# Turning the weights of a step before the product two steps back, in a differential-attention stage

## The chip, the cores and the metric

The kernel runs on one core of a Trainium2 chip. The metric is the device time of one execution in microseconds. The time before is 4780.38 us, the median of three runs (4776.41 to 4782.08).

## The reference, cut to what matters

One layer of a streaming encoder: a combined input projection, a convolution with a state-space scan, differential attention, a mixing projection, a product-key retrieval and a final norm. The change lies in the attention alone, which is this, for 8 heads, 1024 prompt frames and 32 sample frames (these with 512 cached keys and values):

```
def diff_scores_apply(q, k, v, q_pos, k_pos, lam):
    s = jnp.einsum('bqhjd,bkhjd->bhjqk', q, k).astype(jnp.float32) * (A_DK ** -0.5)
    dist = jnp.abs(q_pos[:, None] - k_pos[None, :]).astype(jnp.float32)
    bias = -alibi_slopes()[:, None, None, None] * dist
    mask = (k_pos[None, :] // CHUNK) <= (q_pos[:, None] // CHUNK)
    a = jax.nn.softmax(jnp.where(mask, s + bias, NEG_INF), axis=-1)
    w = a[:, :, 0] - lam * a[:, :, 1]
    return jnp.einsum('bhqk,bkhd->bqhd', w.astype(v.dtype), v)
```

Each head has two score maps (j = 0, 1); their two softmaxes are subtracted to one matrix w of weights, which multiplies the values. All is float32.

## The kernel before, in words

The program is a row of stages, each closed by a barrier of all engines (`Stage.__exit__`): constants, projection and scan, attention (`differential_attention`), then `retrieve_and_finish`. The attention's output rows go to a scratch tensor in memory, and the last stage's first loads are issued behind the barrier.

In the attention stage every engine runs a loop of its own, with four passes of two heads (b = 0, 1). A pass has STEPS = 18 steps m. In a head, steps n = m % 9 from 0 to 7 are the eight tiles of 128 prompt frames, with (n + 1) * 128 keys each, so the tiles grow from 128 to 1024 keys; n = 8 is the sample tile, 32 frames with 544 keys. A step goes through these parts, for which the text below has short names:

- S(m), `scores` on TensorE (L1342; L1348 and L1349 for the sample tile): the two score maps into PSUM. S holds one tile for each map, so the scores of map j wait until VectorE has read map j of the step before (`biased[j]`).
- B(m), `bias_and_max` on VectorE (L1214, L1218): bias, running maximum, copy to SBUF.
- E(m), `exps` on ScalarE (L1260): the two exponentials and their sums.
- W(m), `combine` on VectorE (L1226, L1228, L1233): the weights w. The last instruction (L1233) waits for the product of step m - 2 (`o_done`), because w has two buffers.
- T(m), `weights_turned` on TensorE (L1360): w is transposed in blocks of 128, in groups of up to four blocks; each group has one of two PSUM tiles, `tp`. It waits for W(m) and, before each group, until ScalarE has emptied that `tp` tile.
- C(m), `weights_out` on ScalarE (L1273, L1275): each group is copied from `tp` to `wT` in SBUF. It waits for T(m) and for the product of step m - 1 (`o_done`), because `wT` has two buffers.
- P(m), `product` on TensorE (L1376): wT times the values into `ob`. It waits for C(m).
- O(m), `o_to_rows` on ScalarE (L1295): `ob` to the output rows.

The keys of each head also are transposed, for the output and the cache: `keys_turned` on TensorE, called K here (four groups through the same two `tp` tiles: two of eight prompt blocks in all at L1324, one small at L1326, one of cached keys at L1329), emptied by `keys_out` on ScalarE (L1284, L1286, L1288). K of the first head stands at the start of a pass, K of the second at m = 8, ahead of S(9).

The order of the work on an engine is its program's order. VectorE: for each m, B(m), then W(m - 1). The other two, before the change:

```
TensorE, step m:  [K if m = 8]  S(m+1)  P(m-2)  T(m-1)
ScalarE, step m:  E(m)  [keys_out if m = 8]  O(m-2)  C(m-1)
```

S is called only while m + 1 < 18, so the last three steps of a pass (m = 17, 18, 19) have no scores on TensorE, and in m = 19 only P(17) and O(17) are left.

Of the kernel before, what the change touches and what calls it, by code (L numbers as in the profile page):

```python
# [1065 lines left out]
def differential_attention(nc, io, dr, c, negdist):  # L1066
# [4 lines left out]
    STEPS = 2 * NT  # L1071
# [17 lines left out]
    with Stage(nc, "attn") as s:  # L1089
# [33 lines left out]
        def step_of(i, m, ahead=1):  # L1123

            return i * STEPS + (m + ahead)

        def turn_val(i, j, ahead=1):
            return i * TURNS + (j // 2 + ahead)

        with nc.Block() as block:  # L1130

            @block.gpsimd
            def _(pool):
                pool.iota(iot[:], [[-1, SEQ]], base=SEQ - P, channel_multiplier=1).then_inc(dist_i, 1)
                with pool.Fori(0, H // 2) as i:
                    for b in range(2):

                        pool.wait_ge(head_used[b], i + 1)
                        pool.sem_inc(gate, 1)
                        col = i * (2 * P) + b * P  # L1140
                        pool.dma_start(qT[b][:], dr["chan"][bass.ds(col, P), :]).then_inc(head_in[b], 16)
                        pool.dma_start(kT[b][:], dr["chan"][bass.ds(col + C_K, P), :]).then_inc(head_in[b], 16)
                        cols = bass.ds(col, P)
                        pool.dma_start(vt[b][:, 0:NPT, :], io["v_prompt_out"].rearrange("(t p) c -> p t c", p=P)[:, :, cols]
                                       ).then_inc(head_in[b], 16)
                        pool.dma_start(vt[b][0:DEC, NPT, :], io["v_sample_out"][:, cols]).then_inc(head_in[b], 16)
                        pool.dma_start(kc[b][:], io["cache_k2"].rearrange("(t p) c -> p t c", p=P)[:, :, cols]
                                       ).then_inc(head_in[b], 16)
                        pool.dma_start(vc[b][:], io["cache_v2"].rearrange("(t p) c -> p t c", p=P)[:, :, cols]
                                       ).then_inc(head_in[b], 16)  # L1150
# [95 lines left out]
            @block.scalar  # L1246
            def _(act):
                for b in range(2):
                    act.sem_inc(head_used[b], 1)
                    act.sem_inc(turn_out[b], 1)  # L1250
                act.sem_inc(o_out, 2)
                act.wait_ge(lam_step, 2)
                act.activation(le[:], ld[:], ACT.Exp).then_inc(lam_exp, 1)

                def exps(i, m):
                    p = m % 2
                    r, W = (P, (m % NT + 1) * P) if m % NT < SAMPLE else (DEC, PAST + DEC)
                    act.wait_ge(ntop_done, step_of(i, m))
                    for j in range(2):
                        act.activation(e[j][p][0:r, 0:W], e[j][p][0:r, 0:W], ACT.Exp, bias=ntop[p][0:r, j:j + 1],  # L1260
                                       scale=AK ** -0.5, accum_out=tot[p][0:r, j:j + 1]).then_inc(exp_done[j], 1)

                def weights_out(i, m):
                    r = P if m % NT < SAMPLE else DEC
                    for g, blocks in enumerate(groups(m % NT)):
                        j = turn_of["w", m, g]
                        act.wait_ge(turned[j % 2], turn_val(i, j))

                        act.wait_ge(o_done, step_of(i, m, 2))
                        full = [q for q in blocks if q[1] == P]  # L1270
                        if full:
                            f = len(full)
                            act.activation(wT[j % 2][:, 0:f, 0:r], tp[j % 2][:, 0:f, 0:r], ACT.Copy).then_inc(turn_out[j % 2], 1)  # L1273
                        else:
                            act.activation(wT[j % 2][0:DEC, 0, 0:r], tp[j % 2][0:DEC, 0, 0:r], ACT.Copy).then_inc(turn_out[j % 2], 1)  # L1275

                def keys_out(i, b):

                    act.wait_ge(stored[b], (i + 1) * 64)
                    for g in range(4):  # L1280
                        j = turn_of["k", b, g]
                        act.wait_ge(turned[j % 2], turn_val(i, j))
                        if g < 2:
                            a = act.activation(krow[b][:, 4 * g:4 * g + 4, :], tp[j % 2][:], ACT.Copy)  # L1284
                        elif g == 2:
                            a = act.activation(krow[b][0:DEC, NPT, :], tp[j % 2][0:DEC, 0, :], ACT.Copy)  # L1286
                        else:
                            a = act.activation(kcT[b][:].rearrange("p (t k) -> p t k", k=P), tp[j % 2][:], ACT.Copy)  # L1288
                        a.then_inc(turn_out[j % 2], 1)

                def o_to_rows(i, m):
                    n, b = m % NT, m // NT
                    r = P if n < SAMPLE else DEC
                    act.wait_ge(o_done, step_of(i, m, 3))
                    act.activation(orow[b][0:r, n, :], ob[m % 2][0:r, 0:P], ACT.Copy).then_inc(o_out, 1)  # L1295
                    if n == SAMPLE:
                        act.sem_inc(head_used[b], 1)

                with act.Fori(0, H // 2) as i:
                    keys_out(i, 0)  # L1300
                    for m in range(STEPS + 2):
                        if m < STEPS:
                            exps(i, m)
                        if m == NT - 1:
                            keys_out(i, 1)
                        if m >= 2:
                            o_to_rows(i, m - 2)
                        if 1 <= m <= STEPS:
                            weights_out(i, m - 1)

            @block.tensor
            def _(pe):
# [19 lines left out]
                def scores(i, m):  # L1332
                    b, n = m // NT, m % NT
                    for j in range(2):

                        hold(pe, pe_gate, biased[j], step_of(i, m))
                        half = slice(AK * j, AK * j + AK)
                        if n < SAMPLE:
                            W = (n + 1) * P
                            for k in range(0, W, 512):  # L1340
                                x = min(W, k + 512)
                                mm = pe.matmul(S[j][:, k:x], qT[b][half, n * P:(n + 1) * P], kT[b][half, k:x],  # L1342
                                               start=True, stop=True)
                        else:
                            jj = turn_of["k", b, 3]

                            hold(pe, pe_gate, turn_out[jj % 2], turn_val(i, jj, 2))
                            pe.matmul(S[j][0:DEC, 0:PAST], qT[b][half, SEQ:T], kcT[b][half, :], start=True, stop=True)  # L1348
                            mm = pe.matmul(S[j][0:DEC, PAST:PAST + DEC], qT[b][half, SEQ:T], kT[b][half, SEQ:T],  # L1349
                                           start=True, stop=True)  # L1350
                        mm.then_inc(scored[j], 1)

                def weights_turned(i, m):
                    r = P if m % NT < SAMPLE else DEC
                    pe.wait_ge(w_done, step_of(i, m, 3))
                    for g, blocks in enumerate(groups(m % NT)):
                        j = turn_of["w", m, g]
                        hold(pe, pe_gate, turn_out[j % 2], turn_val(i, j))
                        for k, (blk, size) in enumerate(blocks):
                            t = pe.transpose(tp[j % 2][0:size, k, 0:r], w[m % 2][0:r, blk * P:blk * P + size],  # L1360
                                             c.ident[0:r, 0:r])
                        t.then_inc(turned[j % 2], 1)
# [17 lines left out]
                with pe.Fori(0, H // 2) as i:  # L1380
                    keys_turned(i, 0)
                    scores(i, 0)
                    for m in range(STEPS + 2):
                        if m == NT - 1:
                            keys_turned(i, 1)
                        if m + 1 < STEPS:
                            scores(i, m + 1)
                        if m >= 2:
                            product(i, m - 2)
                        if 1 <= m <= STEPS:  # L1390
                            weights_turned(i, m - 1)


def attend(nc, io, dr, c):
# [1358 lines left out]
```

## Time and profile before

| | |
|---|---|
| median of three runs | 4780.38 us (4776.41 to 4782.08) |
| the profiled execution's own time | 4776.41 us |
| its span in the profile | 4774.6 us |
| mean granted TensorE clock over the span | 0.959 of full speed |
| busy over the span: TensorE, VectorE, ScalarE, GpSimd | 89%, 65%, 21%, 31% |
| attention stage | about 1293 to 1609 us of the span |

How to read it: times inside the span are counted from its start, in microseconds. Busy shares over the whole span are an average over stages with different limits, so the stage of the change is read by itself. A line of the timeline gives the start, the duration and the engine of an instruction, or of a run of equal instructions merged into one (x is how many), and in brackets how long the engine stood idle before it and what ended the wait. A float32 matmul has two records. The ends of matmuls are modelled, so an end can lie a tenth of a microsecond behind the start of the next matmul.

### The profile page before, as it was taken

The numbers are of one execution on the slowest core, as the hardware profiler recorded it, in microseconds if no ns is written. First come the engines' busy times: TensorE is split into PE (matmuls) and PEld (weight loads), VectorE is DVE, ScalarE is ACT, GpSimd is POOL, SyncE is SP. The second block draws the span as 40 slices with busy tenths as digits, with TensorE's granted clock in tenths as the row PEclk, the third lists the DMA queues.
The fourth block names the chain that finished last, engine by engine and source line by source line (L and its number), as shares of the span: only waits on it lengthen the run. The fifth ranks groups of instructions, "written<-read, shape, count | busy, mean of one in ns | idle before, by whom it ended". The sixth has DMA issues, their size and how long they took to land.

```text
span 4774.6 us, 50482 instructions
## 1 busy us (share of the span) xinstructions
PE 4259.6 (89%) x16837; PEld 2648.3 (55%) x16837; DVE 3115.7 (65%) x7131; ACT 996.6 (21%) x2577; POOL 1473.6 (31%) x1391
## 2 busy tenths in 40 slices
PE   7999999999899789988888999878988888888978
PEld 7999777888765675445444555423433433434432
DVE  3444113666377438887788777677777777777784
ACT  2222111234266201111111111111212111212212
POOL 1100001222111003444444344443444444444442
PEclk8999999999899999999999999999999999999999
DMA  2223222344322359999999999999999999999996
GB/s 93 69 88 124 88 90 82 116 132 131 103 82 81 116 188 357 395 413 408 417 406 406 399 419 408 416 420 398 407 409 418 384 404 417 398 412 407 384 414 254
DMA packets 310424, 1379.13 MB, mean 289 GB/s; under 512 B 37856, under 2 KB 112336, under 8 KB 175024
## 3 DMA queue, kind: packets, MB, share of 16 engines
q0 software_dynamic: 167728, 1166.48, 60.5%
q1 hardware_dynamic: 142464, 209.70, 12.7%
q8 instruction: 128, 2.10, 0.2%
q14 instruction: 104, 0.85, 0.0%
HBM read 1295.58 MB, written 80.49 MB: 288 GB/s over the span
## 4 chain that ended last, share of the span: by engine, by line
PE 31%; DMA 20%; DVE 10%; issue 4%; POOL 1%; ACT 0%; SPq 0%; DVEq 0%; ACTq 0%; POOLq 0%
DMA peer_uv<-in_peer_uv_dram,peer_idx 20%; PE peer_acc L2655 18%; PE peer_fo L2596 4%; PE peer_fo L2609 2%; PE peer_fo L2508 2%; DVE peer_uv L1954 2%; PE peer_tb L2461 2%; DVE peer_diag L1984 1%; POOL peer_uv L1821 1%; PE peer_fo L2518 1%; DVE peer_hot L1912 1%; DVE peer_hot L1915 1%; DVE peer_sel L1918 1%; PE peer_sb L2471 0%; DVE peer_pos L1902 0%
## 5 line engine op out<-in xcount | busy, mean ns | idle before, releaser
L2655 PE MATMUL peer_acc<-peer_uv,peer_diag 128*128 128x512 f32 (+1 forms) x4000 | 1932.1, 621 | 300.9 <-DVE peer_diag L1984 294.3
L1821 POOL DMA_INDIRECT peer_uv<-in_peer_uv_dram,peer_idx x1056 | 1224.9, 1160 | 1718.0 <-PE peer_acc L2655 1598.3
L1954 DVE CUSTOM_DVE_ANT_0 peer_uv<-peer_uv,peer_h 128x1024 f32<-128x1024 f32 x1056 | 1290.5, 1222 | 636.8 <-DMA peer_uv<-in_peer_uv_dram,peer_idx 633.4
L2655 PEld LDWEIGHTS peer_acc<-peer_uv,peer_diag 128*128 128x128 f32 (+1 forms) x4000 | 741.5, 194 | 1281.8 <-issue 726.3
L2420 ACT ACTIVATE peer_ge<-peer_pre 128x1 f32<-128x1 f32 x1056 | 212.7, 203 | 2425.1 <-DVE peer_pre L1954 2413.6
L2596 PE MATMUL peer_fo<-peer_space 128*128 128x256 f32 (+2 forms) x1152 | 395.1, 475 | 43.4 <-DVE peer_space L2048 18.3
L99 PE MATMUL proj_bank<-proj_hTh,proj_wplead 128*128 128x352 f32 x1008 | 357.1, 354 | 0.0
L1984 DVE TENSOR_SCALAR peer_diag<-ident,peer_ge,peer_gw 128x128 f32<-128x128 f32 x968 | 332.2, 343 | 10.3 <-ACT peer_ge L2420 8.2
L2596 PEld LDWEIGHTS peer_fo<-peer_space 128*128 128x128 f32 x1152 | 220.7, 196 | 204.9 <-issue 158.2
L100 PE MATMUL proj_bank<-proj_hTr,proj_wplead 128*128 128x352 f32 x1008 | 328.1, 326 | 0.0
L101 PE MATMUL proj_bank<-proj_hTh,proj_wprest 128*128 128x352 f32 x1008 | 328.0, 325 | 0.0
L99 PEld LDWEIGHTS proj_bank<-proj_hTh,proj_wplead 128*128 128x128 f32 x1008 | 192.7, 191 | 23.0 <-issue 22.4
L89 DVE CAST proj_wplead<-proj_wp 128x4096 fp32r<-128x4096 f32 (+1 forms) x14 | 31.0, 2217 | 260.8 <-DMA proj_wp<-in_w_in_dram 126.2
L100 PEld LDWEIGHTS proj_bank<-proj_hTr,proj_wplead 128*128 128x128 f32 x1008 | 192.3, 191 | 15.6 <-issue 15.6
L101 PEld LDWEIGHTS proj_bank<-proj_hTh,proj_wprest 128*128 128x128 f32 x1008 | 192.0, 191 | 0.0
L2609 PEld LDWEIGHTS peer_fo<-peer_space 128*128 128x128 f32 (+1 forms) x1152 | 141.2, 185 | 66.0 <-issue 61.2
L2609 PE MATMUL peer_fo<-peer_space 128*128 128x128 f32 (+1 forms) x1152 | 147.8, 279 | 19.5 <-DVE peer_space L2061 9.9
L2461 PEld LDWEIGHTS peer_tb<-peer_hT,peer_wq 128*128 128x128 f32 x1152 | 146.1, 200 | 32.0 <-issue 29.2
L759 ACT ACTIVATE proj_stg<-proj_bank 128x352 f32<-128x352 f32 (+2 forms) x117 | 57.7, 495 | 486.5 <-PE proj_bank L101 486.5
L2461 PE MATMUL peer_tb<-peer_hT,peer_wq 128*128 128x128 f32 x1152 | 145.8, 283 | 0.7 <-ACT peer_hT L2259 0.7
L1214 DVE CUSTOM_DVE_ANT_0 attn_e<-attn_S,bias_negdist 128x128 f32<-128x128 f32 (+5 forms) x144 | 103.0, 750 | 63.3 <-PE attn_S L1342 55.3
L336 POOL TENSOR_TENSOR proj_scan<-proj_shared,proj_wdec 128x512 f32<-128x512 f32 (+1 forms) x36 | 37.7, 1048 | 286.2 <-PE proj_yh L1019 241.2
(360 smaller groups left out, 5424.9 us busy)
## 6 DMA issues: line engine op xcount, KB each, us to landing
proj_wp<-in_w_in_dram POOLq DMA_DIRECT2D x13, 2048.0 KB, 9.8
peer_space<-in_w_ssm_o_dram SPq DMA_DIRECT2D x48, 512.0 KB
peer_uv<-in_peer_uv_dram,peer_idx POOLq DMA_INDIRECT x1056
proj_wp<-in_w_in_dram POOLq DMA_DIRECT2D x14, 1024.0 KB, 8.2
peer_space<-in_w_attn_o_dram SPq DMA_DIRECT2D x24, 512.0 KB
peer_space<-in_w_out_dram SPq DMA_DIRECT2D x24, 512.0 KB
scratch_xtok<-proj_shared SPq DMA_DIRECT2D x20, 512.0 KB, 3.2
scratch_chan<-proj_stg SPq DMA_DIRECT2D x48, 176.0 KB, 1.8
```

What stands on the lines that cost most here:

```text
L99: pe.matmul(out, a.bitcast(F32R), b.bitcast(F32R), start=(k == 0), stop=False)
L100: pe.matmul(out, a.bitcast(F32R), br.bitcast(F32R), start=False, stop=False)
L101: mm = pe.matmul(out, ar.bitcast(F32R), b.bitcast(F32R), start=False, stop=(k == last))
L1214: dve.tensor_tensor_reduce(e[j][p][0:r, 0:W], S[j][0:r, 0:W], negdist[0:r, off:off + W], 1.0, -3.0e38, ALU.add, ALU.max, top[p][0:r, j:j + ...
L1821: pool.indirect_dma_start(uv[k][:], None, io["peer_uv"], bass.IndirectOffsetOnAxis(ap=idx[t % 2][:, col:col + 1], axis=0)).then_inc(uv_in[ ...
L1954: dve.tensor_tensor_reduce(uv[k][:, 0:D], uv[k][:, 0:D], h2[t % 2][:], 1.0, 0.0, ALU.mult, ALU.add, pre[g % 2][:, k:k + 1]).then_inc(u_don ...
L1984: dve.tensor_scalar(diag[k][:, 0:r], c.ident[:] if r == P else fold[:], ge[g % 2][:, k:k + 1], gw[t % 2][:, it * SLOTS + k:it * SLOTS + k ...
L2420: act.activation(ge[g % 2][:, k:k + 1], pre[g % 2][:, k:k + 1], ACT.Gelu_apprx_tanh).then_inc(gelu_done, 1)
L2461: x = pe.matmul(tb[h // 4][:, h % 4, :], wq[:, k, h * P:(h + 1) * P], hT[:, k, :], start=(k == 0), stop=(k == DK - 1))
L2596: x = pe.matmul(bank[n % 2][:, 0:e], w[q % WR][:, k, :], xb[p % 2][:, k, 0:e], start=(k == 0), stop=(k == CB - 1))
L2609: x = pe.matmul(bank[n % 2][0:r, i * P:(i + 1) * P], sm[:, k, inside(i, r)], w[q % WR][:, k, :], start=(k == 0), stop=(k == CB - 1))
L2655: x = pe.matmul(acc[0:r, h:h + HALF], diag[k][:, 0:r], uv[k][:, D + h:D + h + HALF], start=(it == 0 and k == 0), stop=False)
```

## The change

On TensorE, T(m - 1) is now called ahead of P(m - 2); on ScalarE, C(m - 1) is called ahead of O(m - 2). Every wait, count, buffer and instruction stays as it was.

```
--- before.py
+++ after.py
@@ -1303,10 +1303,10 @@
                             exps(i, m)
                         if m == NT - 1:
                             keys_out(i, 1)
+                        if 1 <= m <= STEPS:
+                            weights_out(i, m - 1)
                         if m >= 2:
                             o_to_rows(i, m - 2)
-                        if 1 <= m <= STEPS:
-                            weights_out(i, m - 1)
 
             @block.tensor
             def _(pe):
@@ -1385,10 +1385,10 @@
                             keys_turned(i, 1)
                         if m + 1 < STEPS:
                             scores(i, m + 1)
+                        if 1 <= m <= STEPS:
+                            weights_turned(i, m - 1)
                         if m >= 2:
                             product(i, m - 2)
-                        if 1 <= m <= STEPS:
-                            weights_turned(i, m - 1)
```

## Rows read from the trace of the kernel before

**Rows 1.** Busy time of each engine in one pass (windows): stretch, length, busy, clock, DMA.
```profile
1380.00:1450.00 70.00, 64.13 (x364) 42.77 (x363) 55.24 (x137) 45.58 (x118) 4.06 (x6) 0.95 0.24 78
```

**Rows 2.** Waits in 1290 to 1600: who waited for whom, us, times, longest.
```profile
DVE attn_e L1214 <- PE attn_S L1342: 55.3, 30, 9.6
...
DVE attn_e L1214 <- DVE attn_w L1233: 7.9, 42, 0.2
```

**Rows 3.** Timeline, the middle of a head: W(13), P(12), S(16), B(16).
```profile
1429.36 0.89 DVE L1233 SCALAR_TENSOR_TENSOR attn_w<-attn_e,attn_inv 128x640 f32<-128x640 f32 x1
...
1430.10 1.16 PE L1376 MATMUL attn_ob<-attn_vt,attn_wT 128*128 128x128 f32 x8
...
1431.74 2.90 PE L1342 MATMUL attn_S<-attn_kT,attn_qT 64*128 64x512 f32 x8
...
1434.87 1.22 DVE L1214 CUSTOM_DVE_ANT_0 attn_e<-attn_S,bias_negdist 128x1024 f32<-128x1024 f32 x1 [0.18 <-DVE attn_w L1233]
```

**Rows 4.** Timeline from the first head's end to the second head's keys, m = 7 and 8.
```profile
1403.79 1.15 DVE L1233 SCALAR_TENSOR_TENSOR attn_w<-attn_e,attn_inv 128x896 f32<-128x896 f32 x1
...
1403.89 1.60 PE L1376 MATMUL attn_ob<-attn_vt,attn_wT 128*128 128x128 f32 x12
...
1405.53 0.28 ACT L1295 ACTIVATE attn_orow<-attn_ob 128x128 f32<-128x128 f32 x1 [0.25 <-PE attn_ob L1376]
...
1405.97 0.98 ACT L1273 ACTIVATE attn_wT<-attn_tp 128x512 f32<-128x512 f32 x2 [0.16 <-PE attn_tp L1360]
...
1406.71 1.07 PE L1324 MATMUL attn_tp<-ident,attn_kT 128*128 128x128 f32 x8 [0.45 <-ACT attn_wT L1273]
...
1408.30 1.05 ACT L1284 ACTIVATE attn_krow<-attn_tp 128x512 f32<-128x512 f32 x2
...
1409.98 0.49 PE L1342 MATMUL attn_S<-attn_kT,attn_qT 64*128 64x128 f32 x4
```

**Rows 5.** Timeline behind these keys, m = 8 to 10.
```profile
1410.41 1.83 PE L1376 MATMUL attn_ob<-attn_vt,attn_wT 128*128 128x128 f32 x14
...
1412.34 0.77 DVE L1233 SCALAR_TENSOR_TENSOR attn_w<-attn_e,attn_inv 32x544 f32<-32x544 f32 x1
...
1413.04 0.70 PE L1342 MATMUL attn_S<-attn_kT,attn_qT 64*128 64x256 f32 x4
...
1413.67 2.05 PE L1376 MATMUL attn_ob<-attn_vt,attn_wT 128*128 128x128 f32 x16
...
1416.04 0.92 PE L1342 MATMUL attn_S<-attn_kT,attn_qT 64*128 64x384 f32 x4
```

**Rows 6.** Timeline of a pass's end and the first keys of the next two passes.
```profile
1441.33 1.80 PE L1376 MATMUL attn_ob<-attn_vt,attn_wT 128*128 128x128 f32 x14 [0.41 <-issue]
...
1442.97 1.28 DVE L1233 SCALAR_TENSOR_TENSOR attn_w<-attn_e,attn_inv 128x1024 f32<-128x1024 f32 x1
...
1444.40 1.07 PE L1360 MATMUL attn_tp<-ident,attn_w 128*128 128x128 f32 x8 [1.27 <-DVE attn_w L1233]
...
1445.76 2.02 PE L1376 MATMUL attn_ob<-attn_vt,attn_wT 128*128 128x128 f32 x16 [0.30 <-issue]
...
1448.18 0.28 ACT L1273 ACTIVATE attn_wT<-attn_tp 128x128 f32<-128x128 f32 x1
...
1448.56 1.03 PE L1376 MATMUL attn_ob<-attn_vc,attn_wT 128*32 128x128 f32 x8 [0.39 <-issue]
...
1449.85 1.09 PE L1324 MATMUL attn_tp<-ident,attn_kT 128*128 128x128 f32 x8
...
1525.07 1.09 PE L1324 MATMUL attn_tp<-ident,attn_kT 128*128 128x128 f32 x8
```

**Rows 7.** The same place as rows 5 in the last pass: timeline, then windows.
```profile
1561.38 3.08 PE L1376 MATMUL attn_ob<-attn_vt,attn_wT 128*128 128x128 f32 x14
...
1565.66 0.70 PE L1342 MATMUL attn_S<-attn_kT,attn_qT 64*128 64x256 f32 x4
...
1560.00:1565.00 5.00, 4.81 (x27) 4.34 (x27) 2.35 (x9) 1.36 (x4) 0.00 (x0) 0.67 0.00 0
```

More of the change, by code:

```diff
@@ L1305, in _ @@
                             keys_out(i, 1)
+                        if 1 <= m <= STEPS:
+                            weights_out(i, m - 1)
                         if m >= 2:
                             o_to_rows(i, m - 2)
-                        if 1 <= m <= STEPS:
-                            weights_out(i, m - 1)
             @block.tensor
@@ L1387, in _ @@
                             scores(i, m + 1)
+                        if 1 <= m <= STEPS:
+                            weights_turned(i, m - 1)
                         if m >= 2:
                             product(i, m - 2)
-                        if 1 <= m <= STEPS:
-                            weights_turned(i, m - 1)
 def attend(nc, io, dr, c):
```

## The prediction

> **What bounds the kernel now.** The change touches one stage, so I read that stage and not the page's shares. The busy times by stretch come first [rows 1]: in 70 us of the attention TensorE shows 64.1 us busy, VectorE 55.2 and ScalarE 45.6. Nothing has much room, so an order can matter, but only where the engine that is reordered is the one the others wait for. The list of waits says how often that is [rows 2]: VectorE's bias pass waits 30 times for scores, 55.3 us in all, and 42 times it starts directly behind its own weights W, 0.2 us each. Of the 72 steps, over half are paced by VectorE and the rest by TensorE. The timeline says which are which; I read it step by step over one pass. From the fourth tile of a head to the end of it VectorE runs without a gap. TensorE sets the pace at two places in a pass: where the first head ends and the second begins (m = 7 to 11), because of the keys and because the longest products and turnings meet the shortest scores; and at the pass's end (m = 16 to 19), where no scores are left. A pass takes 75.2 us (1449.85 to 1525.07 [rows 6]).
>
> **What the change moves.** It adds and removes no instruction. T(m-1) has to wait for W(m-1), the newest thing that VectorE makes; P(m-2) has to wait only for C(m-2), which is old. Before, P ran while VectorE finished W. Now P is queued behind T. Behind P's signal stand C(m-1) on ScalarE and the last instruction of W(m) on VectorE, which both wait for P(m-2). On ScalarE, O(m-2) moves behind C(m-1), but C could not start ahead of P(m-2)'s end anyway; what moves is that E(m+1) and the key copies, next in ScalarE's queue, now stand behind all of C and O, none of which runs beside T any more.
>
> **Middle of a head: about nothing.** In the step of rows 3, W(13) ends at 1429.36 + 0.89 = 1430.25, and P(12) started at 1430.10. A matmul starts 0.15 us behind the VectorE instruction that it waits for (W(16) ends at 1442.97 + 1.28 = 1444.25, T(16) starts at 1444.40 [rows 6]). So T(13) starts at 1430.40 in the place where P(12) started at 1430.10, and the next scores S(16) are 0.3 us late. They were there for both maps at 1431.74 + 2.90 = 1434.64, and VectorE takes up the first map at 1434.87 and the second 1.22 us later [rows 3]: the second has over a microsecond of slack, and the first is done well ahead of 1434.64, since both are in that record. The delay is not carried on, for T waits for VectorE each time. The cover is VectorE's own pass; if it were gone, the price would be 0.3 us in each of the 42 steps, 13 us. The first tiles of a pass wait for VectorE anyway, and P(0) and P(1) are short: nothing.
>
> **First crossing (m = 7, 8): +1.8 us.** In m = 7 TensorE has only the short sample scores, so it is early and W(6) late, ending at 1403.79 + 1.15 = 1404.94 [rows 4]. Before, P(5) filled that time, 1403.89 to 1405.49. Now T(6) starts at 1404.94 + 0.15 = 1405.09. Eight turnings have a record of 1.07 us [rows 6], whose last tenth the next matmul overlaps, so seven take 0.86; P(5) follows at 1405.95 and ends 1.60 later at 1407.55. O(5) started 0.04 behind P(5)'s end [rows 4], so C(6) is released at 1407.59 and not at 1405.97. From C(6) to the key copies it was 1408.30 - 1405.97 = 2.33 us; now O(5) stands between, 0.2 of whose 0.28 us don't overlap the next: 2.53, so the key copies start at 1410.12, and S(9) 1.68 behind them (1409.98 - 1408.30) at 1411.80, against 1409.98: +1.82. The keys' first eight turnings can start 0.74 behind C (1406.71 - 1405.97), at 1408.33, early enough.
>
> **Behind the keys (m = 8 to 10): +0.6 us more.** With S(9) at +1.82, T(7) does not wait; T(7) and P(6) fill the same time as before in the other order, so S(10) starts at 1413.04 + 1.82 = 1414.86, and P(6), now last, ends 0.17 behind that, at 1415.03 (an overlap of a tenth or two, as everywhere). W(8), which before started at 1412.34, just behind P(6) (1410.41 + 1.83 = 1412.24 [rows 5]), again has P(6) as its last wait, now with T(7) ahead of it: it runs 1415.13 to 1415.90. T(8) can start at 1416.05, but TensorE was free at 1414.86 + 0.63 = 1415.49 (the distance from S(10) to P(7)). T(8) and P(7) take 1416.04 - 1413.67 = 2.37 us in either order, so S(11) starts at 1418.42: +2.38. The next steps keep this distance, and VectorE takes over the pace at S(13). The place costs **2.4 us**.
>
> **Pass's end (m = 16 to 19): +2.5 us.** Before, P(15) filled the time in which W(16) was made, 1441.33 to 1443.13, with 1.27 us still idle ahead of T(16) at 1444.40 [rows 6]. Now T(16) starts at the same 1444.40 and P(15) only 0.98 behind it: 1445.38 to 1447.20. On this wait W(17), 1447.30 to 1448.08 (0.77 long like W(8) [rows 5]), and C(16), 1447.24 to 1448.34 (0.98 for seven blocks in rows 4, some 1.1 for eight). T(17) waits for W(17), 1448.23, and its second group for the second copy, 1448.49. So P(16) starts at about 1448.65 and ends 2.02 later at 1450.67, C(17) is released at 1450.71, P(17) follows 0.38 behind it (1448.56 - 1448.18) at 1451.09, and the next pass's keys 1.29 behind that (1449.85 - 1448.56) at 1452.38: +2.53. Part of the loss of P(15) comes back here already: T(17) no longer lies between P(16) and C(17), nor O(16) ahead of C(17).
>
> **Sum at an unchanged clock.** 2.4 + 2.5 = 4.9 us a pass; four passes: **19.6 us**. The last pass's share goes straight into the stage's end, since the barrier and the last stage's loads stand behind the last output rows.
>
> **The clock.** TensorE stands idle for about 2 us ahead of T(16) now, and at the keys about half a microsecond longer than before. In the last pass the granted clock fell at the keys: 0.67 of full speed as the mean of 1560 to 1565, so 1.2 GHz for part of it and 2.4 for the rest [rows 7]. P(6) took 3.08 us in place of 1.83, and S(10) came 1565.66 - 1561.38 = 4.28 us behind it in place of 2.63: a fall costs 1.65 us. It came in one pass of four, at gaps that were alike in all. With longer gaps at eight places I count three falls in place of one, two more: 3.3 us. Bounds: none more (0, or -1.65 if the present one goes), and seven more: 11.6 us, or up to 20 if a fall at the pass's end also slows P(16), the longest product.
>
> The Trainium skill (TensorE: Matmul & The Clock Gate, "HAM oscillation") ties such a fall to a long gap without matmuls. By it the short gaps counted here would leave the clock alone, and the sum would stay at 19.6. Rows 7 speak against it: no gap at that place can have been longer than from the end of the keys' first eight turnings to S(9), 1407.78 to 1409.98 in the like place of rows 4, and five more turnings lie inside.
>
> 19.6 + 3.3 = 22.9 us. On the profiled execution's 4776.41 us this gives 4799.3; that run was the fastest of three, 4.0 us under the median. Against the median it is 4780.4 + 22.9 = **4803.3 us**, 0.48% more. A measurement of this kernel can tell some 0.2%, 9.6 us, from no change.
>
> **Rivals.**
>
> The loss is mostly taken up: slack that I don't see hides part of it. For it speaks that most of the stage is paced by VectorE. It would need the pass's end to cost nothing, which leaves 4 x 1.8 = 7 us: 4788, within 0.2%. Against it: no scores are left there that could hide P(15). Chance 0.13, with the case that the edit does nothing at all (4780).
>
> The middle is not covered: the 0.3 us count in the 42 steps, or E comes late behind C and O and VectorE waits for it. 19.6 + 13 = 33 us, and 36 with the two falls: 4816. For it: TensorE shows 64 of 70 us busy. Against it: in those steps part of this is the second map's scores waiting for VectorE. Chance 0.12.
>
> The clock falls at nearly every crossing: 19.6 + 11.6 to 20, 4812 to 4820. Chance 0.13.
>
> No further fall: gaps of this length leave the clock alone, 19.6 us, 4800. Chance 0.25; it lies within the main case's range. It is what the rule on the clock above would have.
>
> Faster: the copy is what TensorE waits for. If ScalarE's order held P up at each step, 0.2 us less of O ahead of C would give 72 x 0.2 = 14 us: 4766. It decides where P starts directly behind C. The rows show P or K waiting so at three places in a pass [rows 4, 6], so it is at most 4 x 3 x 0.2 = 2.4 us, which the sum has in part. Chance 0.05.
>
> **How the numbers follow.** Main case, 4794 to 4811: 0.32 for about two more falls and 0.25 for none, 0.57 together. The uncovered middle and the cold crossings hold 0.25 above it, the covered case 0.13 and the faster one 0.05 below. The range runs from 4789 to 4817; it leaves out the faster case, most of the covered one and the top of the two upper ones, 0.2. Slower 0.82, within 0.2% 0.13, faster 0.05.
>
> **What the changed profile would show.** T(6) 0.15 us behind W(6), P(5) after it, and S(9) 1.8 us later against W(6) than before; at a pass's end about 2 us of idle ahead of T(16) and P(15) behind it; W(17) waiting for P(15) and W(8) for P(6); a pass of 80.1 us plus 1.65 for each fall; bias passes in the middle of a head still 0.2 us behind W; every other stage as long as before. I am wrong if a pass stays under 77 us, if the middle steps stretch, or if the clock falls at more than four of the eight places.

## The result, and the profile after

The changed kernel takes 4807.24 us (median of five, 4805.06 to 4809.05), against 4780.38 before: a ratio of 1.0056, 95% interval 1.0043 to 1.0069, so 26.9 us or 0.56% slower. The forecast was 4803.3 us, in a range of 4789 to 4817. The profiled execution of the changed kernel took 4809.42 us, 2.2 us over the median; that of before was 4.0 us under it, so the two traces differ by 33 us and not by 27.

```profile
span 4807.7 us, 50478 instructions
```

Who waited for whom in the attention stage of the changed kernel, 1290 to 1640 us (us in total, times, longest), against [rows 2]:

```profile
ACT attn_wT L1273 <- PE attn_ob L1376: 118.5, 68, 4.9
...
DVE attn_e L1214 <- PE attn_S L1342: 58.2, 26, 9.7
PE attn_tp L1360 <- DVE attn_w L1233: 32.1, 54, 2.4
...
DVE attn_w L1233 <- PE attn_ob L1376: 21.2, 13, 3.1
...
DVE attn_e L1214 <- DVE attn_w L1233: 8.7, 46, 0.2
```

The new waits are those that the queues imply. In 54 places TensorE now stands in front of T until VectorE has written w, 32.1 us; before, that wait had 5 places and 5.4 us. ScalarE's copy C waits for the product, 118.5 us; in the middle of a head that delays nothing (see below), but at the crossing the keys stand behind this copy, and there it is part of the loss. VectorE waits for products 13 times, 21.2 us in all (before 5 times, 2.3 us). Yet the bias pass still starts 46 times directly behind its own weights: the middle of the heads has not changed.

The timeline of the first crossing, in the last pass, where the clock stayed up (start, duration, engine, operation, idle time before it and its releaser). These rows answer to [rows 4] and [rows 5]:

```profile
1575.01 1.15 DVE L1233 SCALAR_TENSOR_TENSOR attn_w<-attn_e,attn_inv 128x896 f32<-128x896 f32 x1
...
1576.31 0.95 PE L1360 MATMUL attn_tp<-ident,attn_w 128*128 128x128 f32 x7 [1.12 <-DVE attn_w L1233]
...
1577.10 1.50 PE L1376 MATMUL attn_ob<-attn_vt,attn_wT 128*128 128x128 f32 x12
...
1578.70 0.98 ACT L1273 ACTIVATE attn_wT<-attn_tp 128x512 f32<-128x512 f32 x2 [1.95 <-PE attn_ob L1376]
1579.45 1.06 PE L1324 MATMUL attn_tp<-ident,attn_kT 128*128 128x128 f32 x8 [0.84 <-ACT attn_wT L1273]
...
1581.19 1.05 ACT L1284 ACTIVATE attn_krow<-attn_tp 128x512 f32<-128x512 f32 x2
1581.81 0.28 PE L1326 MATMUL attn_tp<-ident,attn_kT 128*32 128x128 f32 x1 [1.30 <-ACT attn_krow L1284]
...
1582.87 0.49 PE L1342 MATMUL attn_S<-attn_kT,attn_qT 64*128 64x128 f32 x4
...
1586.06 0.77 DVE L1233 SCALAR_TENSOR_TENSOR attn_w<-attn_e,attn_inv 32x544 f32<-32x544 f32 x1 [0.90 <-PE attn_ob L1376]
...
1589.38 0.92 PE L1342 MATMUL attn_S<-attn_kT,attn_qT 64*128 64x384 f32 x4
```

W(6) ends at 1576.16 and T(6) starts 0.15 us later; P(5) stands behind it and ends at 1578.60, C(6) has waited for it for 1.95 us, and the keys wait for C(6). S(9) comes 6.71 us behind W(6)'s end, where it was 5.04 (1409.98 - 1404.94): +1.67. W(8) waits 0.90 us for P(6). S(11) comes 13.22 us behind W(6)'s end, and it was 11.10: +2.12.

The end of the second pass, which answers to [rows 6]:

```profile
1456.61 1.06 PE L1360 MATMUL attn_tp<-ident,attn_w 128*128 128x128 f32 x8 [2.36 <-DVE attn_w L1233]
...
1457.51 1.73 PE L1376 MATMUL attn_ob<-attn_vt,attn_wT 128*128 128x128 f32 x14
1459.34 1.08 ACT L1273 ACTIVATE attn_wT<-attn_tp 128x512 f32<-128x512 f32 x2 [2.41 <-PE attn_ob L1376]
1459.35 0.77 DVE L1233 SCALAR_TENSOR_TENSOR attn_w<-attn_e,attn_inv 32x544 f32<-32x544 f32 x1 [1.58 <-PE attn_ob L1376]
1460.27 0.48 PE L1360 MATMUL attn_tp<-ident,attn_w 32*128 32x32 f32 x5 [1.03 <-DVE attn_w L1233]
...
1464.45 1.09 PE L1324 MATMUL attn_tp<-ident,attn_kT 128*128 128x128 f32 x8
```

TensorE is idle for 2.36 us ahead of T(16), with P(15) ready behind it. From T(16) to the next pass's keys it is 7.84 us, where it was 5.45: +2.39. Again W(17) waits for P(15) (1.58 us), and T(17) for W(17).

One step in the middle of a head, the same as [rows 3], in the second pass:

```profile
1442.60 0.74 PE L1360 MATMUL attn_tp<-ident,attn_w 128*128 128x128 f32 x5 [0.21 <-DVE attn_w L1233]
...
1443.18 1.06 PE L1376 MATMUL attn_ob<-attn_vt,attn_wT 128*128 128x128 f32 x8
...
1444.16 2.68 PE L1342 MATMUL attn_S<-attn_kT,attn_qT 64*128 64x512 f32 x8
...
1447.08 1.22 DVE L1214 CUSTOM_DVE_ANT_0 attn_e<-attn_S,bias_negdist 128x1024 f32<-128x1024 f32 x1 [0.18 <-DVE attn_w L1233]
```

T(13) waits for W(13), P(12) follows, S(16) starts 1.71 us behind W(13)'s end, where it was 1.49 (1431.74 - 1430.25 [rows 3]), and B(16) still starts 0.18 us behind the weights. From W(12)'s start to W(16)'s end it takes 18.74 us in all four passes before and in three of the changed kernel's; the fourth shows 18.76.

Most of what is left of the difference is the granted clock. The crossing of the second pass, timeline and windows, against [rows 5] and [rows 7]:

```profile
1420.16 1.97 PE L1360 MATMUL attn_tp<-ident,attn_w 128*128 128x128 f32 x8
...
1421.92 2.90 PE L1376 MATMUL attn_ob<-attn_vt,attn_wT 128*128 128x128 f32 x14
```

```profile
1420.00:1425.00 5.00, 5.00 (x28) 4.72 (x26) 1.42 (x8) 0.21 (x2) 0.00 (x0) 0.56 0.00 0
```

Here T(7) takes 1.97 us and P(6) 2.90, where they take 1.09 and 1.73 at 2.4 GHz (the last pass): most of 1420 to 1425 was at 1.2 GHz. TensorE had been idle for 1.12, 0.84 and 1.30 us ahead of it, in front of T(6), of the keys and of their third group.

The first pass shows that one crossing can have two such stretches, with the full clock between them (T(6), P(5), the keys' first groups and third group, T(7), then windows):

```profile
1328.54 1.48 PE L1360 MATMUL attn_tp<-ident,attn_w 128*128 128x128 f32 x7 [1.12 <-DVE attn_w L1233]
1329.82 2.66 PE L1376 MATMUL attn_ob<-attn_vt,attn_wT 128*128 128x128 f32 x12
1333.32 1.07 PE L1324 MATMUL attn_tp<-ident,attn_kT 128*128 128x128 f32 x8 [0.84 <-ACT attn_wT L1273]
1335.68 0.39 PE L1326 MATMUL attn_tp<-ident,attn_kT 128*32 128x128 f32 x1 [1.30 <-ACT attn_krow L1284]
...
1337.93 1.97 PE L1360 MATMUL attn_tp<-ident,attn_w 128*128 128x128 f32 x8
```

```profile
1329.00:1332.00 3.00, 3.00 (x16) 3.00 (x15) 2.57 (x8) 0.00 (x0) 0.00 (x0) 0.50 0.02 5
1332.50:1335.50 3.00, 1.07 (x8) 0.86 (x8) 1.28 (x1) 2.93 (x8) 0.00 (x0) 1.00 0.00 0
1336.00:1342.00 6.00, 5.92 (x28) 5.29 (x28) 1.35 (x7) 0.97 (x3) 0.00 (x0) 0.50 0.00 0
```

The first stretch began within T(6), before the gaps of 0.84 and 1.30 us; it slowed T(6) and P(5), the second T(7) and P(6).

The same marks can be read in all passes, as start and end of the instructions of L1233. The table gives the distance from W(6)'s end to W(9)'s start, and from W(16)'s end to W(17)'s end, pass by pass; it holds the later runs as well (C marks a piece in which the clock fell. In the new order a crossing near 15.0 us had one short stretch at 1.2 GHz, one near 16.2 a longer one, and one near 18 had both).

| kernel | W(6) to W(9), four passes | W(16) to W(17), four passes |
|---|---|---|
| before | 10.89, 10.89, 10.89, 12.54 (C) | 1.46, 1.47, 1.46, 1.46 |
| changed | 17.97 (C), 16.17 (C), 15.02 (C), 13.40 | 3.66, 3.66, 3.65, 4.85 (C) |
| changed_again | 13.39, 13.40, 13.39, 13.40 | 5.29 (C), 5.28 (C), 5.29 (C), 5.28 (C) |
| pe_alone | 18.10 (C), 13.45, 13.45, 16.27 (C) | 3.65, 5.29 (C), 5.30 (C), 3.66 |
| act_alone | 11.05 in each | 1.46, 1.46, 1.45, 1.46 |
| crossing_only | 18.01, 17.93, 17.85, 17.80 (all C) | 1.46, 1.46, 1.47, 1.46 |
| end_only | 10.89, 10.89, 10.89, 10.95 | 3.66, 3.66, 3.67, 3.66 |
| middle_only | 10.89 in each | 1.46 in each |
| filler | 15.04 (C), 13.40, 13.40, 13.40 | 3.66 in each |
| filler_again | 13.40, 13.41, 13.39, 13.40 | 3.66, 3.65, 3.65, 3.66 |

With the clock up, a pass pays 13.40 - 10.89 = 2.51 us at the crossing, of which 0.39 comes back by W(12) (W(9) to W(12) 9.29 us, before 9.68), and 3.66 - 1.46 = 2.20 at its end, with 0.19 more until W(0) of the next pass (10.41, before 10.22). That is 2.12 + 2.39 = 4.51 us a pass, 18.0 us in all.

The attention from its first W to its last product (these ends from the same timelines) is 297.9 us before (1304.60 to 1602.53) and 326.1 changed (1303.50 to 1629.60): +28.2. Of this 18.0 is the order. The falls at the three crossings are 4.57 + 2.77 + 1.62 us (against 13.40), the one in the last pass's end is 1.19 us up to W(17) and some 2.7 behind it (7.14 us from W(17) to the last product's end, where the other passes need 4.4 from W(17), 1460.12 in the second, to the next keys, 1464.45), less the 1.65 that before had itself: 11.2. The first half heads (W(0) to W(6)) were 1.1 us shorter.

These first half heads hide falls that the table leaves out. In the kernel before, too, the clock was at 1.2 GHz at the start of the second, third and fourth pass, where the tiles are short and TensorE waits for VectorE again and again; this is the second's:

```profile
1381.00:1387.00 6.00, 5.60 (x13) 3.14 (x15) 4.84 (x16) 3.52 (x12) 0.00 (x0) 0.50 0.94 317
```

Every trace of the case has such a stretch at the start of these three passes, with one exception (the last pass of keys_behind, below). The part from W(0) to W(6) takes 22.9 us there and 23.3 to 25.0 us in the other passes of the runs with the keys at m = 8.

The other 5 us between the two traces lie outside the stage, in front of it -1.1 and behind it +6.0. Behind it the changed_again trace shows 3169.3 us (1635.6 to 4804.9), the first one 3178.1 and before 3172.1, so that part is what executions differ by, and not the change. In front of the stage the traces differ as much: its first W starts between 1303.50 and 1314.06.

### The profile page after: what moved, and what is told of

Same layout as the page of the kernel before. It is cut to its first block, busy times and chain, and to the rows that moved or that the text cites. A ratio compares the mean times of both kernels' runs of the same rounds, so it can differ in the third digit from the quotient of the medians.

```text
span 4807.7 us, 50478 instructions
## 1 busy us (share of the span) xinstructions
PE 4270.5 (89%) x16837; PEld 2668.8 (56%) x16837; DVE 3116.6 (65%) x7131; ACT 987.1 (21%) x2577; POOL 1462.2 (30%) x1391
## 4 chain that ended last, share of the span: by engine, by line
PE 32%; DMA 19%; DVE 10%; issue 4%; POOL 1%; ACT 0%; SPq 0%; DVEq 0%; ACTq 0%; POOLq 0%
PE peer_acc L2655 19%; DMA peer_uv<-in_peer_uv_dram,peer_idx 19%; PE peer_fo L2596 4%; PE peer_fo L2609 3%; PE peer_fo L2508 2%; DVE peer_uv L1954 2%; PE peer_tb L2461 2%; DVE peer_diag L1984 1%; DVE peer_hot L1915 1%; DVE peer_hot L1912 1%; DVE peer_sel L1918 1%; PE peer_fo L2518 1%; POOL peer_uv L1821 0%; PE peer_sb L2471 0%; DVE peer_x L1965 0%
## 5 line engine op out<-in xcount | busy, mean ns | idle before, releaser
L2461 PEld LDWEIGHTS peer_tb<-peer_hT,peer_wq 128*128 128x128 f32 x1152 | 147.5, 202 | 32.1 <-issue 29.3
```

The costliest lines, as they stand in the source:

```text
L2461: x = pe.matmul(tb[h // 4][:, h % 4, :], wq[:, k, h * P:(h + 1) * P], hT[:, k, :], start=(k == 0), stop=(k == DK - 1))
```

## The experiments

The theory was the prediction's: the loss comes from TensorE's queue alone, at two places of a pass, with the granted clock on top. The first rival puts half of it or more on ScalarE's order, the second spreads it over all steps.

**One engine at a time.** In pe_alone only TensorE has the new order, in act_alone only ScalarE.

```
 # pe_alone: TensorE only          # act_alone: ScalarE only
+weights_turned(i, m - 1)         +weights_out(i, m - 1)
 product(i, m - 2)                 o_to_rows(i, m - 2)
-weights_turned(i, m - 1)         -weights_out(i, m - 1)
```

> Only TensorE's order is changed: T(m-1) ahead of P(m-2); ScalarE keeps O(m-2) ahead of C(m-1). Queue theory (P stands behind a turning that waits for VectorE, at two places of a pass, and the granted clock falls in some of the gaps): the whole loss is here already, about 18 us for the order and 7 to 10 for more falls of the clock, 4803 to 4809 us. ScalarE theory (half or more of the loss comes from the copies, the exponentials and the key copies standing behind one another on ScalarE): at most half of 27 us, 4780 to 4794 us.

> Only ScalarE's order is changed: C(m-1) ahead of O(m-2); TensorE keeps P(m-2) ahead of T(m-1). Queue theory: O adds 0.2 us ahead of E(8) once a pass and takes about as much away ahead of C(17): 4779 to 4782 us, no change. ScalarE theory: 4793 us or more.

Measured: pe_alone 4808.37 us, ratio 1.0052 (1.0038 to 1.0065); act_alone 4782.13 us, ratio 1.0000 (0.9991 to 1.0009), both beside a before of 4782.67. TensorE's order is the whole loss. In act_alone O behind C adds 0.16 us at each crossing (11.05 against 10.89), too little to measure in the whole. Beside TensorE's new order, ScalarE's gives something back: from W(17) to the next W(0) it is 10.68 us in pe_alone and 10.41 in the changed kernel, about 1 us over the four passes. The ScalarE rival falls.

**One place at a time.** Both engines' orders are changed, but only in some steps m of a pass; the line shown stands for both engines.

```
-if 1 <= m <= STEPS: weights_turned(i, m - 1)   # ahead of the product, in all steps
+if (m in (7, 8, 9, 10)) and 1 <= m <= STEPS: weights_turned(i, m - 1)     # crossing_only
+if (m in (16, 17, 18)) and 1 <= m <= STEPS: weights_turned(i, m - 1)      # end_only
+if (m not in (7, 8, 9, 10, 16, 17, 18)) and 1 <= m <= STEPS: weights_turned(i, m - 1)  # middle_only
 product(i, m - 2)
```

> Both orders are changed, but only in the steps m = 7 to 10 of a pass. Queue theory: 2.1 us in each of four passes is 8.5 us, and with the falls of the clock that this place had in the changed kernel's profile (8.5 us, less the 1.6 of before) some 15 us: 4790 to 4797 us, and the passes' ends as before. If the loss were spread over all steps, this would have 4 of 18 steps' share of it, 6 us: 4786 us.

> Both orders are changed, but only in the steps m = 16 to 18. Queue theory: 2.4 us in each of four passes is 9.6 us, and up to 3 us for one fall of the clock: 4789 to 4794 us. If the loss were spread over all steps, 3 of 18 steps' share of it, 4.5 us: 4785 us.

> Both orders are changed in all steps but m = 7 to 10 and m = 16 to 18. Queue theory: VectorE sets the pace there and covers the 0.3 us by which the products start late: 4778 to 4783 us, no change. Spread theory (each step loses a little, or the loss is in what the last stage does after a stage that ends otherwise): 4785 us or more.

Measured: crossing_only 4805.89 us, ratio 1.0043 (1.0030 to 1.0057); end_only 4794.35 us, 1.0030 (1.0019 to 1.0042), both beside 4782.67; middle_only 4781.51 us, 1.0001 (0.9992 to 1.0009), beside 4783.67. Of the 17 steps in which both calls occur (m = 2 to 18), ten can be turned round for nothing that can be measured (within 0.09%, 4 us), three at the end cost 0.3%, and four at the crossing 0.43%. The second rival falls. (The ratios are not the quotients of the medians, which are 1.0024 for end_only and 1.0049 for crossing_only.)

The crossing cost more than was expected of it, 0.43% or 20.6 us (23.2 by the medians) against 15, and the two places together more than the whole change. The table says why: in the traced execution of crossing_only, the longest of its five, the clock fell twice at each of the four crossings, together 4.5 us a time. These are the windows of 14 us around them:

```profile
1339.00:1353.00 14.00, 11.28 (x56) 9.43 (x55) 5.13 (x15) 5.24 (x13) 0.00 (x0) 0.66 0.00 0
1421.00:1435.00 14.00, 11.46 (x57) 9.68 (x55) 5.30 (x15) 5.26 (x13) 0.00 (x0) 0.67 0.00 0
1503.00:1517.00 14.00, 11.47 (x59) 9.70 (x57) 5.40 (x15) 5.24 (x13) 0.00 (x0) 0.67 0.00 0
1585.00:1599.00 14.00, 11.42 (x59) 9.65 (x57) 5.41 (x15) 5.29 (x13) 0.00 (x0) 0.67 0.00 0
```

A mean of 0.67 between two levels of 1.0 and 0.5 is two thirds of the 14 us at 1.2 GHz. With 2.12 us for the order and 4.5 for the clock, minus the one fall of before, this sums to 4 x 2.12 + 18.0 - 1.65 = 24.8 us, and the stage's trace is 24.9 us longer (1312.54 to 1635.33). In end_only the falls came elsewhere, at T(15) and P(14) of three passes, 0.8 us each. T(15) follows short sample scores and a gap of 1.12 us, as T(6) does, and the prediction had not counted it among the places of a fall.

**The gaps filled.** The changed kernel, with turnings of the identity in TensorE's gaps; they write a part of a PSUM tile that nothing reads, and the rest is computed as before. It was run twice, the second time on one chip with the changed kernel (changed_again).

```
+def filler(i, n, m):
+    pe.wait_ge(o_out, step_of(i, m, 3))
+    for _ in range(n):
+        pe.transpose(ob[m % 2][:, 256:256 + P], c.ident[:], c.ident[:])
 for g in some groups of keys_turned(i, 1):
+    if g in (0, 2): filler(i, 6 if g == 0 else 9, 4)
...
+if m == STEPS - 1: filler(i, 14, 13)
 weights_turned(i, m - 1)
```

> The changed kernel, with turnings of the identity into an unused part of a PSUM tile put in TensorE's new gaps: 6 ahead of the second head's keys, 9 ahead of their third group, 14 ahead of T(16), some 0.12 us each, so that the gaps are filled and little is delayed; nothing reads them. Clock theory (about 10 us of the 27 are further falls of the granted clock, caused by these gaps): no fall at the eight places, 4795 to 4799 us. If the falls cost nothing or do not come from the gaps: 4806 to 4810 us.

> The changed kernel once more, beside the next run on the same chip: 4804 to 4810 us. In its trace W(6) to W(9) is 13.4 us where the clock stays up (2.1 us more than before, less than what a later piece gives back) and more where it falls; which passes see the fall may differ from the first profile.

> The changed kernel with its gaps filled by turnings that nobody reads, on the same chip as the run before. Clock theory: the attention stage 7 to 10 us shorter than the changed kernel's, and so the median, unless the last stage differs by itself. If the falls do not come from the gaps: the same median within 3 us.

Measured: filler 4803.70 us, ratio 1.0041 (1.0028 to 1.0054), beside a before of 4783.67. On one chip, beside 4783.97: changed_again 4808.11 us, 1.0050 (1.0037 to 1.0064), and filler_again 4801.38 us, 1.0032 (1.0021 to 1.0043). More work on the busiest engine makes the kernel 6.7 us faster. The median of filler moved less than was expected of it (4795 to 4799), and that of filler_again stays just under the 7 to 10 us expected. From the first W to the last product it is 316.3 us in filler (1304.19 to 1620.49) and 315.3 in filler_again (1308.41 to 1623.73), where the changed kernel had 326.1 and 321.6: the stage is 10 and 6 us shorter. Behind the stage filler's trace shows 3184.7 us, the longest of all. The windows of filler_again over its crossings:

```profile
1334.00:1348.00 14.00, 12.94 (x104) 10.64 (x103) 7.97 (x26) 7.61 (x25) 0.00 (x0) 1.00 0.00 1
1415.00:1429.00 14.00, 12.94 (x101) 10.25 (x101) 7.94 (x27) 7.92 (x26) 0.00 (x0) 1.00 0.00 0
...
1576.00:1590.00 14.00, 12.94 (x98) 9.65 (x95) 7.94 (x26) 8.52 (x28) 0.00 (x0) 1.00 0.00 0
```

The clock stays at 2.4 GHz through all of them, and all four distances are 13.39 to 13.41 us, which is the crossing of the new order without a fall. The stage is 17.4 us longer than that of before (315.3 against 297.9), close to the 18.0 of the order alone, and so is the median (4801.38 against 4783.97). No fall began at a filled gap in either trace. One crossing of eight still fell, in T(6) of filler's first pass, ahead of the first filling (15.04), and three pieces from W(12) to W(16), where nothing was filled, took 19.5 us in place of 18.74, again at T(15) and P(14); at the starts of the passes the clock fell as in the other traces. In changed_again the falls are at the passes' ends, in every one, and none at a crossing; in the first profile of the same kernel they were at three crossings and one end. So the same gaps do not decide alone where the clock falls.

**Something to gain at the crossing.** If TensorE's waits are what the crossing costs, then work put into them should be worth something. In keys_spread the second head's four key groups are turned and copied one by one at m = 3 to 6. In keys_behind the keys are turned later: K behind S(0) at a pass's start, and S(9), P(6), K, T(7) at m = 8; keys_behind_product has the second half of that alone. All start from the kernel before; the waits for the head's data move with the first use of them, and in keys_spread the turns of the `tp` tiles follow the new order.

```
 # keys_spread: one group a step, on both engines
-if m == NT - 1: keys_turned(i, 1)
+if m in (3, 4, 5, 6): keys_turned(i, 1, [(3, 4, 5, 6).index(m)])
 # keys_behind
-keys_turned(i, 0)
 scores(i, 0)
+keys_turned(i, 0)
...
-if m == NT - 1: keys_turned(i, 1)          # keys_behind_product: from here on
 if m + 1 < STEPS: scores(i, m + 1)
 if m >= 2: product(i, m - 2)
+if m == NT - 1: keys_turned(i, 1)
```

> The order of before, but the four key groups of the second head are turned and copied one by one at the start of the steps m = 3, 4, 5 and 6, not together at m = 8. If the middle steps have room on TensorE and ScalarE, the 3.7 us between the end of T(6) and S(9) go in each pass, and with the clock's one fall there some 15 us: 4764 to 4770 us. If they have none (TensorE busy, VectorE waits for scores that stand behind a key group), the time comes back in these steps: 4776 to 4784 us.

> The order of before, but TensorE turns the keys later: at a pass's start K behind S(0), not ahead of it, and at m = 8 in the order S(9), P(6), K, T(7). If TensorE's waits at these places are what a pass pays for: at the crossing P(6) fills the waits for the copy and for E(8) (0.45 + 1.14 us), at the pass's start VectorE's first bias pass runs beside the keys (S(1) comes 1.1 us sooner): 2.7 us in each of four passes and the clock's fall at the keys, 4768 to 4774 us if before is at 4781. If the key copies, which stay where they were on ScalarE, set the end of K either way: within 3 us of before.

> Only the crossing's part of that: S(9), P(6), K, T(7) at m = 8. From W(6)'s end to W(9), 10.9 us before, about 1.6 us less in each pass, 6 us and the clock's fall there: 4773 to 4778 us if before is at 4781. If ScalarE sets the end of K: no change.

Measured: keys_spread 4780.99 us, ratio 0.9997 (0.9989 to 1.0006), beside 4783.67; keys_behind 4773.19 us, 0.9980 (0.9971 to 0.9989); keys_behind_product 4777.01 us, 0.9987 (0.9978 to 0.9996), both beside 4783.97. So keys_behind beats both kernels of the case, before by 0.2%. Both medians of the keys_behind pair lie in the ranges given for them, but not by the sums behind these, as the traces show below.

keys_spread was a miss, and its trace shows why. W(6) to W(9) fell from 10.89 to 8.9 us in each pass, but W(0) to W(6) rose from between 24.2 and 25.0 to between 25.9 and 27.9. This is m = 3 of its second pass (line numbers are one higher than before's):

```profile
1389.04 1.11 PE L1325 MATMUL attn_tp<-ident,attn_kT 128*128 128x128 f32 x4 [1.10 <-DMA attn_vc<-in_cache_v_dram]
1390.09 2.51 PE L1343 MATMUL attn_S<-attn_kT,attn_qT 64*128 64x512 f32 x8
...
1392.89 0.82 DVE L1215 CUSTOM_DVE_ANT_0 attn_e<-attn_S,bias_negdist 128x640 f32<-128x640 f32 x1 [3.41 <-PE attn_S L1343]
```

The second head's data had not landed, TensorE waited 1.10 us for them with S(4) in its queue behind, at the lower clock, and VectorE stood still for 3.41 us. The last three passes have such a wait; the first has none and lost least (25.9 against 25.0). That the middle steps can hide 0.3 us, as in middle_only, does not say that they can hide a key group.

In keys_behind the crossing shrank by 0.5 us (10.37), not by 1.6, and the way from W(17) to the next W(0) by 0.56 (9.66), not by 1.1. The rows are W(7), K from its first group to its third, T(7) and S(10):

```profile
1411.04 1.28 DVE L1233 SCALAR_TENSOR_TENSOR attn_w<-attn_e,attn_inv 128x1024 f32<-128x1024 f32 x1
1411.41 1.04 PE L1324 MATMUL attn_tp<-ident,attn_kT 128*128 128x128 f32 x8
...
1412.76 0.28 PE L1326 MATMUL attn_tp<-ident,attn_kT 128*32 128x128 f32 x1 [0.31 <-ACT attn_krow L1284]
...
1414.68 0.63 PE L1360 MATMUL attn_tp<-ident,attn_w 128*128 128x128 f32 x4 [0.34 <-ACT attn_kcT L1288]
1415.24 0.70 PE L1342 MATMUL attn_S<-attn_kT,attn_qT 64*128 64x256 f32 x4
```

P(6) now hides the waits for C(6) and E(8), but T(7) stands right behind the keys, and its second group waits 0.34 us until ScalarE has emptied the `tp` tile of the cached keys; the key groups themselves wait 0.31 and 0.21 us for copies in the same timeline. The crossing is then 4 x 0.5 = 2 us, the passes' starts 3 x 0.56 = 1.7, and the stage is 7.0 us shorter in its trace (290.9 against 297.9). The rest is the fall of the clock that before had (1.65) and shorter first half heads (W(0) to W(6): 96.8 us in sum against 98.3): in its last pass the clock stayed at 2.4 GHz at the start, and W(0) to W(6) took 22.9 us. keys_behind_product has the 2 us of the crossings and the 1.65, and its stage is 3.8 us shorter (294.2). The medians fell by 10.8 and 7.0 us, some 3 us more than the stages in both; where these come from is not shown.

## Why the prediction was right

By its own steps:

- *Middle of a head: about nothing.* Right: 18.74 us from W(12) to W(16) in both, and middle_only has a ratio of 1.0001.
- *First crossing: +1.8 us.* Measured 1.67 in the pass without a fall. P(5) ran 1.50 us there, not 1.60, and ScalarE needed 2.49 us from C(6) to the key copies, not 2.53.
- *Behind the keys: +0.6 us more*, 2.4 in all. Measured 2.12 up to S(11), by the wait that was named: W(8) on P(6), 0.90 us.
- *Pass's end: +2.5 us.* Measured 2.39, again with the two named waits, W(17) on P(15) and T(17) on W(17).
- *Sum at an unchanged clock: 19.6 us.* Measured 4 x 4.51 = 18.0, and filler_again shows it nearly alone: 17.4.
- *The clock: 3.3 us, two falls more at 1.65.* This is the term that was mis-sized. The first profile has 11.2 us of it: falls at four of the eight places (the most that the prediction allowed) where before had one, at 1.6 to 4.6 us each. changed_again has four falls of 1.63 in the passes' ends, from W(16) to W(17), 6.5 us less the 1.65 of before, so 4.9. One fall in the trace of before had been taken as the price of all, and it was a short one in a stretch where TensorE is busy. A short stretch costs about 1.6 us there (T(6) and P(5), T(7) and P(6), or T(16) and P(15)), 0.8 where VectorE has slack to take up a part (T(15) and P(14)); a longer one at the keys costs 2.8, the long one over the last pass's end 3.9 (1.19 + 2.7), and 4.5 us are two stretches at one crossing. The rival "the clock falls at nearly every crossing" is what crossing_only did.
- *"One pass of four".* The clock of before was read at the crossing alone. It also falls at the start of three passes, and [rows 1] has it: a mean of 0.95 over 70 us is 7 us at 1.2 GHz. These falls are in both kernels, so they add little to the difference, but they move the stage by a microsecond or two from one execution to the next.
- *The rival that pays only for the crossing* took 4 x 1.8 = 7 us for it; by the prediction's own 2.4 us it is 9.6, and 4790. This changes no bound of the range.

The terms together are 18.0 + 5 to 11, less about 1 for the first half heads in the first profile. The median moved by 26.9 us in the first set of runs and by 24.1 beside changed_again (4808.11 - 4783.97). The forecast was 4.0 us low. That it came so near is in part luck: the order was priced 1.6 us too high and the clock up to 7.9 too low, and they have opposite signs.

The Trainium skill's rule on the clock (TensorE: Matmul & The Clock Gate, "HAM oscillation") would have left out the falls. The trace disagrees with it as the prediction read it: at the crossings that fell, TensorE's gaps were 1.12, 0.84 and 1.30 us, with work between them. The same section advises to gather TensorE's work ahead of a wait, so that its clock stays up. The traces of filler, in which no fall began at a filled gap, agree with the aim, though the work here was useless and not gathered.

What stays open is what decides at which of several like places the clock falls. The same kernel fell at crossings in one execution and at passes' ends in another.

## What to carry to other kernels

Where a queue's operations run in their program's order, as here, an operation that waits for the newest result should stand behind those whose inputs are old; turned round, it costs only where the engine is ahead of its supplier and nothing else covers the wait, and there it costs about the length of the ready work behind it. (T(15) waits 1.12 us like T(6), but VectorE sets the pace there, and W(12) to W(16) is as long as before.) Find these places in the timeline (here two in a pass, in 7 of 17 steps) rather than multiplying by the number of steps, and look for the second and third waits on the delayed operation's signal. Where new gaps on TensorE arise, price the falls of the clock by their spread and not by one example, and look through the whole stage for those that are there already.

## What the runs showed of the hardware

The granted clock fell to 1.2 GHz after gaps of TensorE of no more than 1.30 us: in the changed kernel's second and third crossing after 1.12, 0.84 and 1.30 us with short work between them, and in its first crossing already in T(6), 1.12 us of idle time and the short sample scores behind it. Gaps of 2.36 us at a pass's end passed without a fall in three of four passes of the first profile, and in none of four in changed_again, the same kernel. In crossing_only, whose last three passes start 82.1 and 82.0 us apart (W(0) at 1395.28, 1477.37 and 1559.38), all four crossings fell alike (17.80 to 18.01 us); in changed_again, with its passes 82.0, 81.8 and 81.9 us apart, all four passes' ends did and no crossing. A stretch at 1.2 GHz cost 0.8 to 3.9 us at these places, by its length and by what TensorE had to do in it. Useless turnings in the gaps, 29 a pass at 0.12 us each, shortened the kernel by 6.7 us.
